# Conv FFN down-projection by Strassen's scheme: where the second direct tile stands in each chunk

## The reference, cut to what matters

```python
FFN_DIM_2 = 3 * D_MODEL      # 3072

def conv_ffn(x, w_up, conv_w, conv_b, w_down):
    u = causal_depthwise_conv(x @ w_up.astype(x.dtype), conv_w, conv_b)
    g, val = jnp.split(u, [FFN_DIM_2], axis=-1)
    return (jax.nn.gelu(g) * val) @ w_down.astype(x.dtype)

        h = h + conv_ffn(rms_norm_2(h, ffn_norm[layer]), ffn_w_up[layer], ...)
```

## Time and profile before

| | before |
|---|---|
| median of three runs | 2985.2 us |
| the profiled execution's own time | 2985.95 us |
| its span, first to last instruction | 2984.1 us |
| TensorE busy | 2929.0 us (98%) |
| VectorE busy | 1584.3 us (53%) |
| GpSimd busy | 1431.2 us (48%) |
| ScalarE busy | 1344.6 us (45%) |
| mean granted clock of TensorE | 0.991 |

### The profile page before, as it was taken

The page is one execution under the profiler, slowest core; times in us unless marked ns, Lnnn a source line. Parts: engine busy times, 40 slices in busy tenths (PEclk is TensorE's granted clock), DMA queues, the critical chain, the costliest instruction groups (busy, mean ns, idle before and its releaser), DMA issues.

```text
span 2984.1 us, 40664 instructions
## 1 busy us (share of the span) xinstructions
PE 2929.0 (98%) x14960; PEld 2425.2 (81%) x14960; DVE 1584.3 (53%) x2504; ACT 1344.6 (45%) x2095; POOL 1431.2 (48%) x827
## 2 busy tenths in 40 slices
PE   9999999999999999999999999999999989999998
PEld 7888888888878888888888877778888777888888
DVE  5667434221073666443221366647676778576757
ACT  4556545222263566453223455545343447443443
POOL 4445355444443654454444353534655542454645
PEclk9999999999999999999999999999999999999999
DMA  4222232223312221323223221113222222222222
GB/s 142 72 92 71 91 121 92 92 97 104 104 67 93 86 92 64 113 94 116 98 93 106 99 81 61 64 62 101 92 91 93 92 78 85 99 92 96 88 99 92
DMA packets 77305, 273.79 MB, mean 92 GB/s; under 512 B 8776, under 2 KB 9416, under 8 KB 77152
## 3 DMA queue, kind: packets, MB, share of 16 engines
q1 hardware_dynamic: 74112, 266.05, 26.9%
q10 hardware_dynamic: 3040, 5.64, 0.5%
HBM read 269.55 MB, written 2.10 MB: 91 GB/s over the span
## 4 chain that ended last, share of the span: by engine, by line
PE 82%; DVE 8%; POOL 4%; ACT 4%; issue 1%; DMA 1%; SPq 0%; DVEq 0%; ACTq 0%; POOLq 0%
PE ps L891 21%; PE ps L893 20%; PE ps L892 20%; DVE XRAW L2940 2%; PE ps L1191 2%; PE ps L1222 2%; PE ps L1169 2%; PE ps L1494 1%; PE ps L1500 1%; PE ps L1495 1%; PE ps L1414 1%; PE ps L1415 1%; PE ps L1416 1%; POOL WLO L3144 1%; PE ps L1295 1%
## 5 line engine op out<-in xcount | busy, mean ns | idle before, releaser
L3144 POOL TENSOR_TENSOR WLO<-WRAW,WHI 128x1024 fp32r<-128x1024 f32 x357 | 864.7, 2425 | 1026.0 <-ACT WHI L1656 1022.4
L891 PE MATMUL ps<-HH,WHI 128*128 128x512 f32 x2144 | 842.7, 393 | 2.3 <-POOL WLO L3144 0.9
L893 PE MATMUL ps<-HH,WLO 128*128 128x512 f32 x2144 | 835.5, 390 | 0.0
L892 PE MATMUL ps<-HL,WHI 128*128 128x512 f32 x2144 | 835.1, 390 | 0.0
L1656 ACT ACTIVATE WHI<-WRAW 128x1024 fp32r<-128x1024 f32 x431 | 452.7, 1051 | 189.4 <-DMA WRAW<-wall 188.3
L891 PEld LDWEIGHTS ps<-HH,WHI 128*128 128x128 f32 x2144 | 403.0, 188 | 91.7 <-issue 5.3
L893 PEld LDWEIGHTS ps<-HH,WLO 128*128 128x128 f32 x2144 | 402.8, 188 | 84.8
L892 PEld LDWEIGHTS ps<-HL,WHI 128*128 128x128 f32 x2144 | 403.1, 188 | 81.0
L2388 DVE TENSOR_TENSOR ACC<-ACC,SQ 128x512 f32<-128x512 f32 x78 | 75.0, 962 | 280.6 <-ACT SQ L1949 271.1
L2906 DVE SCALAR_TENSOR_TENSOR ps<-U,COLS,ps 128x512 f32<-128x512 f32 x192 | 145.1, 756 | 85.2 <-ACT ps L2123 81.7
L3249 POOL TENSOR_SCALAR SG<-SG,RS 128x512 f32<-128x512 f32 (+3 forms) x104 | 109.2, 1060 | 140.6 <-DVE RS L2668 140.6
(11 more groups left out here) (459 smaller groups left out, 5902.7 us busy)
## 6 DMA issues: line engine op xcount, KB each, us to landing
WRAW<-wall SPq DMA_DIRECT2D x502, 512.0 KB, 3.4
y<-X ACTq DMA_DIRECT2D x8, 256.0 KB, 2.2
X<-xin SPq DMA_DIRECT2D x3, 512.0 KB, 7.7
DFT<-dft ACTq DMA_DIRECT2D x4, 258.0 KB, 4.4
PT_IN<-pin ACTq DMA_DIRECT2D x2, 512.0 KB, 3.7
DIL<-dil ACTq DMA_DIRECT2D x1, 768.0 KB, 4.2
X<-xin SPq DMA_DIRECT2D x2, 256.0 KB, 4.6
COLS<-cols ACTq DMA_DIRECT2D x1, 290.5 KB, 5.5
```

Of the source, the lines that this page charges most:

```text
L891: pe.matmul(out_, WHI[w_at], x_hi, start=first, stop=False)
L892: pe.matmul(out_, WHI[w_at], x_lo, start=False, stop=False)
L893: return pe.matmul(out_, WLO[w_at], x_hi, start=False, stop=last)
L3144: pool.tensor_tensor(WLO[:, s, :], whole, WHI[:, s, :].bitcast(F32), ALU.subtract).then_inc(wt_lo, 1)
```

## The change

The list of units of a down stage now has both direct tiles, 0 and 1, at its head and the three pairs (tiles 2 and 3, 4 and 5, 6 and 7) behind them. TensorE makes all rows of tile 0 but the last, two rows of tile 1, the last row of tile 0, the other six rows of tile 1, and then the pairs. The other engines follow: the additions of the two direct tiles, the sums of weight blocks, and in the last stage of layer 0 the closing of tiles 0 and 1, which now stands behind the splitting of the seventh unit.

```diff
-def pair_order(pairs, blocks):
-
-    return [None] + [(p, b) for p in range(pairs) for b in range(blocks)] + [None]
+def down_order(blocks):
+
+    pairs = [(t, b) for t in range(2, DT, 2) for b in range(blocks)]
+    return [(0, None), (1, None)] + pairs
...
-SUMS = {who: {n: q for q, n in enumerate(n for n in PAIRED if (UNITS[n][4] == P) == (who == "pool"))} for who in ("pool", "vector")}
+SUMS = {who: {n: q for q, n in enumerate(n for n in PAIRED if (UNITS[n][4] == 2 * P) == (who == "pool"))} for who in ("pool", "vector")}
...
+        def finished_at(st, j):
+
+            if not st.last or j < 3:
+                return ()
+            return (0, 1) if j == 3 else tiles_done(st, j - 1)
...
                 weights(st.unit(0))
                 pe.wait_ge(bank_free[st.bank(0)], st.use(0))
-                direct(0, 0, range(kt - 1))
+                direct(0, range(kt - 1))
+                weights(st.unit(1))
+                pe.wait_ge(bank_free[st.bank(1)], st.use(1))
+                direct(1, range(2))
+                direct(0, range(kt - 1, kt)).then_inc(unit_used, 1)
+                direct(1, range(2, kt)).then_inc(unit_used, 1)
                 for j, p, b in paired_steps(st):
                     if p == 1 and b == 0:
-                        pe.wait_ge(bank_free[st.bank(0)], st.use(4))
-                        for k in range(1, 4):
-                            pe.wait_ge(bank_free[st.bank(k)], st.use(k))
+                        for k in range(4):
+                            pe.wait_ge(bank_free[st.bank(k)], st.use(4 + k if k < 2 else k))
...
-                    if j == 1:
-                        direct(0, 0, range(kt - 1, kt)).then_inc(unit_used, 2)
-                    else:
-                        mm.then_inc(unit_used, 1)
-                j = len(order) - 1
-                weights(st.unit(j))
-                pe.wait_ge(bank_free[st.bank(3)], st.use(7))
-                direct(j, 3, range(kt)).then_inc(unit_used, 1)
-
+                    mm.then_inc(unit_used, 1)
...
             def down(st):
                 for j in range(st.units):
                     split_of(st, j)
-                    if st.last and j:
-                        for t in tiles_done(st, j - 1):
-                            finished(st, t)
+                    for t in finished_at(st, j):
+                        finished(st, t)
...
+            def added(st, j):
+                if direct_at(st, j) is not None:
+                    direct_added(st, direct_at(st, j), j)
+                if ended_at(st, j) is not None:
+                    pair_added(st, ended_at(st, j))
+
             def down(st):
                 for j in range(st.units):
-                    p = ended_at(st, j - 1)
-                    if j == 2:
-                        direct_added(st, 0, 0, 0)
-                    if p is not None:
-                        pair_added(st, p)
+                    added(st, j - 1)
                     sums_of(st, j)
-                    if st.last and j:
-                        for t in tiles_done(st, j - 1):
-                            finished(st, t)
-                direct_added(st, DT - 1, st.units - 1, 3)
+                    for t in finished_at(st, j):
+                        finished(st, t)
+                added(st, st.units - 1)
```

More of the change, by code:

```diff
@@ L99 @@
 PAIR_STEPS = 7
-PAIRS = 3
 A12, A11, A22, A21 = range(4)
@@ L184, in conv_ffn @@
                 product("ffn_w_up_2", l, DM, FFN2 + n * P)
-            for n, unit in enumerate(pair_order(PAIRS, m // 2)):
-                if unit is None:
-                    u.append(("ffn_w_down_2", l, 2 * k0 * P, 2 * m * P, (DT - 1) * P if n else 0, P))
+            for t, b in down_order(m // 2):
+                if b is None:
+                    u.append(("ffn_w_down_2", l, 2 * k0 * P, 2 * m * P, t * P, P))
                 else:
-                    u.append(("ffn_w_down_2 paired", l, k0 + 2 * unit[1], 2, (1 + 2 * unit[0]) * P, 2 * P))
+                    u.append(("ffn_w_down_2 paired", l, k0 + 2 * b, 2, t * P, 2 * P))
     for c in range(6):
@@ L433, in conv_ffn @@
                 per |= {"operand_hi_ready": DT, "operand_ready": DT, "square_ready": DT, "square_added": DT}
-            add("down", 1, PAIRS * m // 2 + 2, 8, per, made=up, heads=PAIRS, last=last, gain=gain)
+            add("down", 1, pairs * m // 2 + 2, 8, per, made=up, heads=pairs, last=last, gain=gain)
     conv_ffn(0, "rec_norm_20")
@@ L808, in order_of, with paired_steps @@
         def order_of(st):
-            return pair_order(st.heads, st.made.reps // 2)
+            return down_order(st.made.reps // 2)
+        def paired_steps(st):
+            return [(j, t // 2 - 1, b) for j, (t, b) in enumerate(order_of(st)) if b is not None]
         def ended_at(st, j):
@@ L815, in ended_at, with direct_at, direct_bank @@
             return next((p for i, p, b in paired_steps(st) if i == j and b == last), None)
-        def paired_steps(st):
-            return [(j, *unit) for j, unit in enumerate(order_of(st)) if unit is not None]
+        def direct_at(st, j):
+            return order_of(st)[j][0] if 0 <= j < st.units and order_of(st)[j][1] is None else None
+        def direct_bank(st, t):
+            return ps[st.bank(t)]
         def tiles_done(st, j):
-            if j == 1:
-                return (0,)
+            if direct_at(st, j) is not None:
+                return (direct_at(st, j),)
             p = ended_at(st, j)
-            return () if p is None else (1 + 2 * p, 2 + 2 * p)
+            return () if p is None else (2 + 2 * p, 3 + 2 * p)
+        def finished_at(st, j):
+            if not st.last or j < 3:
+                return ()
+            return (0, 1) if j == 3 else tiles_done(st, j - 1)
         def pair_bank(p, b):
@@ L1376, in down, with direct @@
             def down(st):
-                up, order = st.made, order_of(st)
+                up = st.made
                 kt, blocks = 2 * up.reps, up.reps // 2
-                def direct(j, k, tiles):
-                    s = st.unit(j) % SLOTS
+                def direct(j, tiles):
+                    s, t = st.unit(j) % SLOTS, direct_at(st, j)
                     for i in tiles:
-                        if j == 0:
+                        if j < 2:
                             pe.wait_ge(S["operand_ready"], up.at("operand_ready", 1 + i % 2, i // 2))
                         row = 4 * (i // 2) + i % 2
-                        mm = three(ps[st.bank(k)][:, :], (slice(None), s, slice(i * P, i * P + P)), FTH[:, row, :], FTL[:, row, :], i == 0, i == kt - 1)
+                        mm = three(direct_bank(st, t)[:, :], (slice(None), s, slice(i * P, i * P + P)), FTH[:, row, :], FTL[:, row, :], i == 0, i == kt - 1)
                     return mm
@@ L2153, in down @@
                 if st.last:
-                    finished(st, DT - 1)
+                    for t in tiles_done(st, st.units - 1):
+                        finished(st, t)
             def finished(st, t):
-                if t in (0, DT - 1):
-                    act.wait_ge(S["direct_added"], st.at("direct_added", 1 if t == 0 else 2))
+                if t < 2:
+                    act.wait_ge(S["direct_added"], st.at("direct_added", t + 1))
                 else:
-                    act.wait_ge(S["pair_step"], st.at("pair_step", PAIR_STEPS * ((t - 1) // 2 + 1)))
+                    act.wait_ge(S["pair_step"], st.at("pair_step", PAIR_STEPS * (t // 2)))
                 if st.gain:
@@ L2983, in pair_added, with direct_added @@
                     dve.wait_ge(S["pair_step"], st.at("pair_step", PAIR_STEPS * p + PAIR_STEPS))
[L2984 removed]
+                    for k, uses in enumerate((1, 1, 2, 2)):
                         dve.engine_nop().then_inc(bank_free[st.bank(k)], uses)
[L2987 removed]
+            def direct_added(st, t, j):
                 dve.wait_ge(unit_used, st.unit(j) + 1)
[L2990 to L2991 removed]
+                dve.tensor_tensor(X[:, t, :], X[:, t, :], direct_bank(st, t)[:, :], ALU.add).then_inc(S["direct_added"], 1)
+                dve.engine_nop().then_inc(bank_free[st.bank(t)], 1)
+            def added(st, j):
+                if direct_at(st, j) is not None:
+                    direct_added(st, direct_at(st, j), j)
+                if ended_at(st, j) is not None:
+                    pair_added(st, ended_at(st, j))
             def down(st):
                 for j in range(st.units):
[L2995 to L2999 removed]
+                    added(st, j - 1)
                     sums_of(st, j)
[L3001 to L3004 removed]
+                    for t in finished_at(st, j):
+                        finished(st, t)
+                added(st, st.units - 1)
                 if st.last:
[L3006 removed]
+                    for t in tiles_done(st, st.units - 1):
+                        finished(st, t)
             def finished(st, t):
```

6 lines of the change are left out of this document (3 added, 3 removed).

## The result

The changed kernel takes 3000.0 us (median of 5 runs, 2996.5 to 3001.8) against 2985.2 (5 runs, 2984.5 to 2985.9). The ratio is 1.0047, 95% interval 1.0035 to 1.006: slower, by 14 to 15 us. The profiled execution has a span of 2998.2 us against 2984.1. The forecast was 2995.5 us, range 2975 to 3006.

What follows compares the result with a forecast made beforehand. TensorE, busy nearly all the time, was taken as the bound. Middle stages +1, program end +4 and end of layer 0 +5.3 gave +10.3: 2996.2 us profiled, 2995.5 as median, range 2975 to 3006.

Steps and rivals of the forecast that it cites:

- The wait at B: Before tiles 4 and 5 in each down stage: wait 4.7, its slow clock 2.5 and an earlier 0.7 go, -7.9 us.
- The head: Start of each down stage: TensorE waits 4.5 us for row 7 of tile 0, then loses 2.5 at lower clock.
- The order of turns: At the stage's start VectorE's four short instructions alternate with GpSimd's, 6.6 us in all, row 7 ready at 2099.1.
- The first rival: Row 7 of tile 0 in time for a short wait, 1.5 us, without lower clock: 2963 us, faster; chance 0.18.
- u7: Eighth unit of a down stage, second of pair C: TensorE waits 1.2 us for its sums, bounds 0 and 2.5.
- the third rival: Wait for the eighth unit also brings lower clock, or head waits 5.5: 1.5 us a stage, 3004 us; chance 0.07.
- the four stages: Down stages followed by an up stage: each costs 8.2 against 7.9 us, +0.3, together +1.
- the load: Seventh unit's weights: 3.8 us from the third unit's end to the seventh's sums, 3.4 of it loading.
- The end of the program: After TensorE's end: copy and seven additions of pair C lie bare, +4 us, range 3 to 5.
- The end of layer 0: Closing tiles before the norm: norm at 2431.8 against 2427.01, +4.8, with lower clock +5.3; bounds -2 and +8.
- half a microsecond more at the lower clock: Behind the norm after layer 0: slower clock following the longer idle time, part of the +5.3 us there.
- The sum: Whole profiled execution: +1 + 4 + 5.3 = +10.3 us, giving 2996.2.

Runs made afterwards that it cites:

- e8: Kernel before the change, with VectorE adding tile 0 ahead of the fifth unit's sums instead of behind them: 2984.7 us, ratio 0.9999.
- e2: Changed kernel, with GpSimd starting the third unit's subtractions only after VectorE has made row 7 of tile 0: 2971.8 us, ratio 0.9955.
- e4: Changed kernel, with the last down stage of each layer back in the order of before: 2988.1 us, ratio 1.0008.
- e9: Kernel of e7, with ScalarE's copy for pair A's addition also moved ahead of its splitting of the seventh unit's weights: 2965.8 us, ratio 0.9937.
- e7: Kernel of e2, with GpSimd also making the fourth unit's sums ahead of its wait for row 7: 2973.8 us, ratio 0.9963.
- e6: Kernel of e2, with VectorE instead of GpSimd making the fourth unit's sums, behind row 7: 2978.4 us, ratio 0.9975.

## Why the prediction came out right

- **The wait at B goes, with its clock (-7.9 a stage).** Right. Its reason was half: it named the addition of tile 0 alone, and e8 shows GpSimd's XLO as a second end, 0.4 us ahead of it.
- **The head (+4.5 and 2.5).** Right in size and cause: 4.5 in each of the six stages, and 1.7 to 2.9, mean 2.4, of lower clock. The order of turns, worked out from two collisions, gave 2099.1 for 2099.31, and e2 shows that the turns decide. The first rival, that VectorE isn't made to take turns, is the kernel that e2 built: 2971.8.
- **u7 (+1.2).** Right in three middle stages (lost 1.3, 1.3, 1.2), too small in one: 2.0 there, with 1.5 of lower clock behind it, which was the third rival's mechanism. So the four stages cost +3.2 for +1. The term that was off there is the load: from the end of u2 to the first of u6's sums the prediction took 3.8 us, and it was 3.8 in the three other middle stages but 4.5 in this one, where u6's weights landed 4.1 us after their issue and not 3.4 or 3.5. TensorE at u7 there, and that load:

```profile
2710.80 0.39 PE L1433 MATMUL ps<-FTH,WHI 128*128 128x256 f32 x1 [1.82 <-POOL XLO L3176]
```
```profile
WRAW<-wall SPq DMA_DIRECT2D x1, 512.0 KB, 4.1
```

- **The end of the program (+4).** +4.6, within its 3 to 5.
- **The end of layer 0 (+5.3).** The norm came at 2431.74, forecast 2431.8; counted from the stage's own start, which was 0.8 us later than before, it is +3.9 for +4.8, so that the two times agree to 0.1 us is luck. The "half a microsecond more at the lower clock" behind it was +2.0: this term was mis-sized most, by a factor of four. Its size is not firm, though: from the norm to the next down stage the kernel before took 232.80 us, and e8, with the same wait of 1.8 us in front of the norm, 231.49.
- **The sum.** 14.1 for 10.3 in the profiled execution. The difference is the middle stages (+2.2), the clock behind the norm (+1.5) and small terms of both signs. The measured 3000.0 lies as near to the third rival's 3004 as to the forecast, and one of the four middle stages shows that rival's slow stretch behind u7.

What stays open: why u6's load in the third middle stage takes 0.7 us longer than in the others, and what of the 2.0 us behind the norm belongs to the longer wait in front of it, since e4 took away the whole end of the stage at once.

## What to carry to other kernels

Before a wait is removed, look at who else ends within half a microsecond of its named releaser (e8), and where the engine that no longer waits will ask next: reordering moved 27 us of waiting to another place, and the gain appeared only when the engines' order behind the new place was changed too (e2, e9). Where VectorE's short SBUF-to-SBUF instructions make an operand that TensorE is about to need, keep GpSimd's long ones away from them, if need be with a wait; here one wait on an engine with slack was worth 28 us.

## What the runs showed that was not expected

- Waits of about equal length were followed by the lower clock in one place and not in another. Heads with 1.8 to 2.0 us lost (e7, e9; 12 of them) ran on at 0.23 us; of e2's waits at u3 with 2.1 us lost, five of six were followed by 1.4 to 1.5 us of slow matmuls; of e6's at u7 in the middle stages (2.3 us lost) two of four. The size of a wait alone did not tell here what the clock would add.
- The granted clock in the 16.7 us behind the norm was 1.00 in e4 with a wait of 0.6 us in front of it, 0.90 before with 1.8, 0.80 after with 3.2, but 0.83 in e2 with 4.7 and 0.90 in e7 with 3.2; in e8, with the 1.8 of before, it was 1.00. Longer idle time did not go with a lower clock throughout, and equal idle time not with an equal one.
